# Twenty-nine matmuls with unused results added where TensorE waits, in a two-layer hybrid retention / SSD / attention step

## What is computed

```
layer 0:  h = modulated rms_norm(x)
          q, k, v, g, z, xbc, dt = split(h @ w_in)
          retention:  8 heads, both directions, chunks of 128 tokens
             y_c = (q_c k_c^T * decay) v_c + q_c S,   S = S * decay + k_c^T v_c
             y = silu(g) * (head_layer_norm(y_fwd + y_bwd) * gain)
          Mamba-2 SSD:  16 heads of 64, state 128, both directions, same recurrence
             with decays that depend on the token
          x += g1 * (concat(y_ret, y_ssm) @ w_out);   x += g2 * conv_ffn(x)
layer 1:  q, k, v = split(h @ w_qkv), rms_norm and rotary positions on q and k
          o = softmax(q k^T / 8) v      16 query heads, 4 key heads
          x += g1 * (o @ w_o);   x += g2 * conv_ffn(x)
```

## Time and profile before

| | |
|---|---|
| median of 3 runs | 1937.83 us (1936.13 to 1939.66) |
| the profiled execution | 1936.91 us |
| its span, first to last instruction | 1935.1 us |
| outside the span | 1.8 us |
| mean granted TensorE clock | 0.995 of full |

### The profile page before, as it was taken

The page is one execution under the profiler, slowest core; times in us unless marked ns, Lnnn a source line. Parts: engine busy times, 40 slices in busy tenths (PEclk is TensorE's granted clock), DMA queues, the critical chain, the costliest instruction groups (busy, mean ns, idle before and its releaser), DMA issues.

```text
span 1935.1 us, 33170 instructions
## 1 busy us (share of the span) xinstructions
PE 1883.0 (97%) x13269; PEld 1797.8 (93%) x13269; DVE 1310.6 (68%) x2143; ACT 864.3 (45%) x1473; POOL 100.5 (5%) x93
## 2 busy tenths in 40 slices
PE   7999999999999999999999999899999999999999
PEld 4998899999988999999999998866699999999999
DVE  4555956666777698788888877666546853663663
ACT  4545742222435466235335445555535641441551
POOL 0000000000010000000000035411100000000000
PEclk8999999999999999999999999999999999999999
DMA  8221014444322233433443331100013222222222
GB/s 314 88 69 44 18 61 131 136 145 150 99 81 76 77 109 120 141 125 100 145 130 117 101 102 58 47 12 1 1 57 107 87 73 69 76 68 84 76 67 74
DMA packets 57066, 175.96 MB, mean 91 GB/s; under 512 B 7552, under 2 KB 9472, under 8 KB 56832
## 3 DMA queue, kind: packets, MB, share of 16 engines
q1 hardware_dynamic: 55152, 172.17, 27.3%
q10 hardware_dynamic: 1808, 2.36, 0.3%
HBM read 170.05 MB, written 4.46 MB: 90 GB/s over the span
## 4 chain that ended last, share of the span: by engine, by line
PE 85%; DVE 8%; ACT 4%; issue 2%; DMA 1%; SPq 0%; POOL 0%; DVEq 0%; ACTq 0%
PE ps L392 74%; PE ps L2269 2%; PE ps L2254 2%; PE ps L982 1%; DVE w_lo L378 1%; DVE PT L2387 1%; DVE x L997 1%; PE ps L2218 1%; PE ps L2217 1%; ACT w_hi L370 1%; DMA modw<-in_w_modA 1%; ACT yv L1873 1%; PE ps L2277 0%; PE ps L1421 0%; PE ps L1753 0%
## 5 line engine op out<-in xcount | busy, mean ns | idle before, releaser
L370 ACT ACTIVATE w_hi<-raw 128x1024 fp32r<-128x1024 f32 (+1 forms) x221 | 230.4, 1043 | 585.3 <-PE ps L392 585.0
L378 DVE TENSOR_TENSOR w_lo<-raw,w_hi 128x1024 fp32r<-128x1024 f32 (+1 forms) x221 | 270.6, 1225 | 300.6 <-ACT w_hi L370 299.9
L392 PE MATMUL ps<-h_hi,w_hi 128*128 128x320 f32 x1392 | 322.5, 313 | 8.6 <-DVE w_lo L378 3.6
L392 PE MATMUL ps<-h_lo,w_hi 128*128 128x320 f32 x1392 | 318.1, 310 | 2.2 <-DVE h_lo L785 1.0
L392 PE MATMUL ps<-h_hi,w_lo 128*128 128x320 f32 x1392 | 317.7, 310 | 0.0
L392 PEld LDWEIGHTS ps<-h_hi,w_hi 128*128 128x128 f32 x1392 | 231.2, 188 | 15.7 <-issue 5.7
L392 PEld LDWEIGHTS ps<-h_lo,w_hi 128*128 128x128 f32 x1392 | 232.7, 188 | 3.2 <-DVE h_lo L785 1.6
L392 PEld LDWEIGHTS ps<-h_hi,w_lo 128*128 128x128 f32 x1392 | 233.0, 188 | 0.0
L392 PE MATMUL ps<-ya_hi,w_hi 128*128 128x320 f32 (+1 forms) x896 | 207.6, 313 | 0.0
L392 PE MATMUL ps<-ya_hi,w_lo 128*128 128x320 f32 (+1 forms) x896 | 205.1, 310 | 0.0
L392 PE MATMUL ps<-ya_lo,w_hi 128*128 128x320 f32 x896 | 204.0, 309 | 0.0
(11 more groups left out here) (311 smaller groups left out, 2985.5 us busy)
## 6 DMA issues: line engine op xcount, KB each, us to landing
raw<-in_ffn_up SPq DMA_DIRECT2D x88, 512.0 KB, 3.5
raw<-in_hyb_in SPq DMA_DIRECT2D x49, 512.0 KB, 4.1
mrawB<-in_w_modB SPq DMA_DIRECT2D x48, 512.0 KB, 4.4
mrawA<-in_w_modB SPq DMA_DIRECT2D x64, 256.0 KB, 2.7
raw<-in_ffn_down SPq DMA_DIRECT2D x32, 448.0 KB, 3.4
raw<-in_hyb_out SPq DMA_DIRECT2D x16, 512.0 KB, 4.2
raw<-in_ffn_down SPq DMA_DIRECT2D x16, 512.0 KB, 3.6
modw<-in_w_modA SPq DMA_DIRECT2D x12, 512.0 KB, 13.2
```

The lines of the kernel that those rows point to most:

```text
L370: act.activation(w_hi[:, i % 2, 0:n], raw[:, b % RAW, 0:n], ACT.Copy).then_inc(S("w_hi"), 1)
L378: eng.tensor_tensor(w_lo[:, i % 2, 0:n], raw[:, b % RAW, 0:n], w_hi[:, i % 2, 0:n].bitcast(F32), SUB).then_inc(S("w_lo"), 1)
L392: last = pe.matmul(pj(f, c1 - c0)[:, hh, :], w[:, i % 2, k * 128:(k + 1) * 128], v[:, k, c0:c1], start=(k == 0 and n == 0), stop=(k == s.K ...
```

## The change

A helper pe_warm(pe, out, n) issues n matmuls of the fp32r identity with itself, the moving side repeated to 512 columns, into a PSUM region that holds nothing needed. No semaphore is waited for or raised, and the results are never read: a later matmul with start=True writes over them.

- In the recurrence: 6, once, for p = 0, between pe_states and pe_decay(p, 2), into bank 6.
- In the retention loop: 3, for p = 0, 1 and 2 (9 in all), behind the first half of the state updates and before the wait for ret_yc, into bank 7.
- In the retention's projection: 7, once, behind the wait for ret_yc and pe_begin of the first output tile and before its first step, into the bank that this tile will use.
- In attention: 4 behind scores(1) and before pe_turn(pe, 11), and 3 behind it, before scores(2), into the bank of scores(0), which had been read.

```diff
+        def pe_warm(pe, out, n):
+            for _ in range(n):
+                pe.matmul(out, ident_r[:, :], ident_r[:, :].unsqueeze(1).to_broadcast([128, 4, 128]), start=True, stop=True)
...
                     pe_states(pe, p)
+                    if p == 0:
+                        pe_warm(pe, B6, 6)
                     pe_decay(pe, p, 2)
...
                     pe_ret_states(pe, p + 1, range(0, 4))
+                    pe_warm(pe, B7, 3)
                     for e in range(2):
                         pe.wait_ge(S("ret_yc"), 2 * p + e + 1)
                         pe_ret_scores(pe, p + 1, (e,))
...
                     pe.wait_ge(S("ret_yc"), 7 + n)
                     pe_begin(pe, s, n)
+                    if n == 0:
+                        pe_warm(pe, flat[:, 1024 * (s.f0 % 2):1024 * (s.f0 % 2) + 512], 7)
...
             scores(1)
+            free = flat[:, 1024 * (f % 2):1024 * (f % 2) + 512]
+            pe_warm(pe, free, 4)
             pe_turn(pe, 11)
             pe.wait_ge(S("ld_vpast"), 16)
             for n in range(N_ATT):
+                if n == 0:
+                    pe_warm(pe, free, 3)
                 if n + 2 < N_ATT:
                     scores(n + 2)
```

## The result

| | before | after |
|---|---|---|
| median, 20 runs each | 1937.65 us (1935.67 to 1939.69) | 1942.49 us (1940.0 to 1944.98) |
| the profiled execution | 1936.91 us | 1943.33 us |
| its span | 1935.1 us | 1941.5 us |
| mean granted clock in it | 0.995 | 0.995 |

The changed kernel takes 1.0024 times as long, 95% interval 1.0018 to 1.003: 4.8 us by the medians, 3.5 to 5.8 us by the interval. It is slower, by 2.9 us more than the 1.96 us forecast. Over all 20 runs the mean granted clock is 0.9952, against 0.9951 to 0.9956 for the kernel before in the five sessions of the experiments. So 29 matmuls meant to hold the clock up did not, as a whole, raise it.

The account below looks back on a forecast made before the run. TensorE was taken to bound the kernel outside a few hand-written stages. 0.55 + 1.65 + 0.60 - 0.84 = +1.96 us on the profiled 1936.91 us gave 1938.9 us, with 8 in 10 from 1935.9 to 1941.8.

Parts of the forecast that it names:

- Recurrence, "I count 0": Recurrence: six matmuls hide in TensorE's wait, the kept clock gives 0 as VectorE works unbroken; far bound 1.3 us gain.
- Retention loop, p = 0, "+0.55": Retention loop, p = 0: no wait there, so the three matmuls partly stick out on the chain, +0.55 us (0.4 to 0.7).
- Loop, p = 2, "-0.84": Retention loop, p = 2: filling half of the 1.35 us wait keeps the clock up for L1769's sixteen matmuls, -0.84 us.
- Projection, "+1.65": Retention's projection: seven matmuls stand behind the release by ScalarE's yv and are paid in full, +1.65 us.
- at half clock, 7 x 0.43 = 3.0 us: Projection: upper bound for the cost of the seven matmuls, should they run at half clock, 3.0 us.
- Attention, "+0.60": Attention: the four fit in a wait, the three before scores(2) make VectorE late, +0.60 us (0.4 to 0.8).
- No clock was lost here in this execution, so nothing is won: Attention: the profiled execution had no fall, so no gain was counted; a later 1.91 us wait stays unfilled.
- What they could protect is not seen: Projection: no clock gain counted for the seven matmuls, since the work behind them is as dense as they are.
- Rival 3: The thirteen added matmuls on the path run at 1.2 GHz, nothing won at p = 2: 1942.5 us, chance 0.08.
- Rival 2: Ordinary executions have more falls in these stages than the profiled one, and filling removes them: 1936.7 us, chance 0.14.
- Rival 1: The clock does not care for filling, half-clock stretches come as before, only cost is left: 1939.7 us, chance 0.20.

Follow-up runs that it names:

- version with all in waits: Against the kernel before, added matmuls only in waits, including six ahead of the projection's wait and six in attention's later wait: 0.9987, in a later session 0.9994.
- path-only kernel: Against the kernel before, only thirteen added matmuls: loop's three for p = 0, projection's seven, three before scores(2): 1.0029, 1942.13 us.

## Why the prediction was wrong, point by point

- **Recurrence, "I count 0".** The six are hidden, and the clock stayed up in the changed kernel's profile, at little gain: the stage is 0.14 us shorter than before. It isn't certain to stay up: 3 of 12 filled profiles fell. Over all profiles a fall costs about 0.4 us there, so some of TensorE's loss seems to reach the end of the stage, and did not lie wholly beside VectorE's unbroken work. The 0 was nearly right, and inside its far bound.
- **Retention loop, p = 0, "+0.55".** A mis-sized term: 0.90 us on the chain. I had let the last matmul of L1769 cover a part, and the three as a group take all of the time from its end to the scores.
- **Loop, p = 2, "-0.84".** Exactly so between the two profiles. But against a median it is not a gain of 0.84: with the loop unfilled the clock fell for p = 2 in 2 of 6 profiles, so a mean over executions holds about a third of it, 0.3 us.
- **Projection, "+1.65".** 1.64 us at full clock: the reasoning about a matmul behind the wait holds. The bound "at half clock, 7 x 0.43 = 3.0 us" was met in other kernels, with 3.09 and 3.35 us on the chain.
- **Attention, "+0.60".** 0.61 us for the matmuls. The term has nothing for the clock behind them.
- **The step that failed** is in two sentences: "No clock was lost here in this execution, so nothing is won", and on the projection "What they could protect is not seen". Both took one execution for the kernel and put the clock at nothing at two places where it falls in other executions: behind attention's later wait, unfilled, in 11 of 13 profiles, and at the projection, unfilled, in 6 of 12. In both profiles of the whole change the fall behind attention's wait cost 2.84 and 2.83 us, against 0.00 in the one profile from which the prediction was made, and all thirteen matmuls on the path ran at full clock. Where a fall meets the seven, as in three other kernels, the projection takes 3.17 to 4.42 us more than with neither, and not 1.64.
- **How far this makes up the 4.8 us.** An estimate from the means of the profiles: the thirteen 3.1 us, those for p = 1 and 2 of the loop 0.1; falls that the filling spares in the recurrence, the loop and attention's earlier wait -0.1, -0.3 and -0.5. At the projection, unfilled, falls cost 1.6 us in the mean over the six kernels with the seven (or 21) and 0.5 over the six without: +1.1. Behind attention's later wait they cost 2.15 us in the mean over the eight unfilled kernels with the three and 0.92 over the five without: +1.2. That is 4.6 us. The last two terms stand on few profiles: falls came in 4 of 6 against 2 of 6, and in 8 of 8 against 3 of 5. That the added matmuls make falls more frequent is not shown.
- **The rivals.** Rival 3 has the measured time, 1942.5 us, and that is luck: it had all thirteen at half clock and nothing won for p = 2, and in both profiles of the whole change the thirteen ran at full clock and no fall came in the loop. In other kernels added matmuls did run at half clock, because of a fall in the wait ahead of them and not as a rule. Rival 2 was right that other executions have more falls, but the two places where they come most often and cost most are the ones that the change leaves unfilled. Rival 1, that the clock doesn't care for filling, goes against the table where the matmuls lie in the wait, most clearly in attention's later wait (11 of 13 against 0 of 6). It describes the whole change well all the same, as the clock's mean didn't move. The Trainium skill, "TensorE: Matmul & The Clock Gate", section "Why this matters for your kernels", warns only of idle gaps longer than any of these. The trace differs: here the clock fell behind waits of 1.1 to 2.4 us, and once, at 558.6 in the kernel with the seven only, behind two of 0.40 and 0.50 us. The measurement decides.
- **Open.** The interval of the 4.8 us alone is 2.3 us wide, and the start of an execution moves it by as much: in both profiles of the whole change the time up to 177.59 us is 1.3 to 1.4 us longer than in the one of the kernel before, which two profiles can't tell from chance. How long a fall behind attention's wait lasts goes with its start: in the four of 6.8 us it came 0.5 to 0.9 us before the wait's end, in the seven of 3.4 us from 0.1 us before the end to 1.6 us behind it. All four have the three added matmuls, but so have four of the seven, so the three by themselves don't make it long.

## What to carry to other kernels

A matmul issued to keep the clock up belongs in front of the semaphore wait, where it costs next to nothing (0.0 to 0.1 us for a group here); behind it, it lengthens the path by its full time, and by up to 1.7 times that when the fall that it should prevent has already come. Here the wait left unfilled was the dearest of the places. Find the waits to fill from several profiles, since one execution shows only some of the falls, and price a fall by the engine that bounds the stage. Even the version with all in waits won 0.13% at most, so a loss of 0.3% is easier to make here than a gain.

## What the runs showed of the hardware

- Half-clock stretches came in lengths of about 3.4, 6.8 and 10.2 us, behind the start nearly all at the same few waits, but not in every kernel's profile: with attention's later wait unfilled in 11 of 13.
- The clock can fall within the idle time, before any matmul follows: it was 0.81 in the microsecond from 603, with TensorE at 0.00 busy throughout, in the path-only kernel.
- Identity matmuls whose results nobody reads run like others: seven of 512 columns take 1.74 us from start to start of the next (604.55 to 606.29), 0.25 us each.
- Executions can be up to 3.3 us apart by 178 us, before the first changed instruction (19 profiles). It goes with the time at half clock in their first 50 us: the seven with 13.7 us (in the changed kernel's profile from 16.3 to 26.5 and 33.4 to 36.8) are 1.1 to 1.8 us later than the kernel before with its 10.2 us, the nine with 6.8 or 3.4 us are 0.5 to 1.5 us earlier.
- How long a fall lasted went with when it began against the end of the wait: 6.8 us where 0.5 to 0.9 us before it, 3.4 us where later (attention, 11 profiles).
